# Three middle norms: later order of the second half, and the inverse root as ScalarE's square root and VectorE's reciprocal

## The reference

```python
def rms_norm(x, g):
    xf = x.astype(jnp.float32)
    y = xf * lax.rsqrt(jnp.mean(xf * xf, axis=-1, keepdims=True) + EPS)
    return (y * g.astype(jnp.float32)).astype(x.dtype)

    x = x + g1[:, None] * mix
    h2 = rms_norm(x, g_ffn_norm[l]) * (1.0 + sc2[:, None]) + sh2[:, None]
    u = causal_depthwise_conv(h2 @ w_up[l], w_conv[l], b_conv[l])
```

## Time and profile before

| what | value |
| --- | --- |
| median of 3 runs | 1750.63 us (1747.38 to 1750.98) |
| the profiled execution, its own time | 1747.48 us |
| its span | 1745.7 us, 32410 instructions |
| TensorE busy | 1691.8 us (97%) |
| VectorE busy | 1092.8 us (63%) |
| ScalarE busy | 744.8 us (43%) |
| GpSimd busy | 298.2 us (17%) |
| mean granted clock of TensorE | 0.994 |

### The profile page before, as it was taken

One profiled execution on the slowest core, in us unless ns is written; L12 is line 12 of the kernel. 1 busy time (PEld: TensorE's weight loads), 2 busy tenths in 40 slices (PEclk: granted clock), 3 DMA queues, 4 the chain that ended last, 5 costly groups with the idle time before them and its releaser, 6 DMA issues.

```text
span 1745.7 us, 32410 instructions
## 1 busy us (share of the span) xinstructions
PE 1691.8 (97%) x12781; PEld 1503.0 (86%) x12781; DVE 1092.8 (63%) x1748; ACT 744.8 (43%) x1111; POOL 298.2 (17%) x286
## 2 busy tenths in 40 slices
PE   5999999999999999899999999999999999999998
PEld 4876666788888888799999999999999999989986
DVE  6866586777664568855858664344753766754633
ACT  4467574455332342632323545446323643322323
POOL 2112296211000002532005221110102000000002
PEclk8999999999999999999999999999999999999999
DMA  9463532443333232263435752332543233332332
GB/s 313 122 145 97 161 114 80 130 91 113 95 91 105 85 103 69 79 182 118 132 102 156 225 142 87 99 117 80 166 117 96 74 96 90 91 97 85 96 95 75
DMA packets 321167, 201.18 MB, mean 115 GB/s; under 512 B 51279, under 2 KB 303814, under 8 KB 320918
## 3 DMA queue, kind: packets, MB, share of 16 engines
q1 hardware_dynamic: 300976, 160.79, 32.4%
q0 software_dynamic: 7952, 24.83, 4.7%
q10 hardware_dynamic: 12118, 13.88, 2.3%
HBM read 177.75 MB, written 17.24 MB: 112 GB/s over the span
## 4 chain that ended last, share of the span: by engine, by line
PE 84%; DVE 6%; ACT 4%; SPq 2%; issue 2%; DMA 1%; POOL 1%; ACTq 0%; DVEq 0%; POOLq 0%
PE ps L1467 69%; SPq L854 2%; PE ps L1769 1%; DVE wlo L2154 1%; PE ps L1608 1%; PE ps L1795 1%; PE ps L1779 1%; PE ps L1667 1%; PE ps L1999 1%; PE ps L1682 1%; PE ps L1584 1%; DVE acol L2229 1%; ACT whi L912 1%; DMA xrow<-in_x_dram 1%; PE ps L1925 0%
## 5 line engine op out<-in xcount | busy, mean ns | idle before, releaser
L1467 PE MATMUL ps<-zhi,whi 128*128 128x258 f32 (+2 forms) x2072 | 639.1, 308 | 1.4 <-ACT ub L1201 0.6
L1467 PE MATMUL ps<-zlo,whi 128*128 128x258 f32 (+2 forms) x2072 | 633.4, 306 | 0.0
L1467 PE MATMUL ps<-zhi,wlo 128*128 128x258 f32 (+2 forms) x2072 | 632.0, 305 | 0.0
L1467 PEld LDWEIGHTS ps<-zhi,whi 128*128 128x128 f32 x2072 | 390.8, 189 | 25.6 <-issue 2.2
L2154 DVE TENSOR_TENSOR wlo<-stage,whi 128x1024 fp32r<-128x1024 f32 x256 | 324.2, 1268 | 136.1 <-ACT whi L912 124.1
L1467 PEld LDWEIGHTS ps<-zlo,whi 128*128 128x128 f32 x2072 | 390.2, 188 | 19.5 <-issue 1.2
L1467 PEld LDWEIGHTS ps<-zhi,wlo 128*128 128x128 f32 x2072 | 390.8, 189 | 18.2
L912 ACT ACTIVATE whi<-stage 128x1024 fp32r<-128x1024 f32 x256 | 269.4, 1055 | 309.3 <-PE ps L1467 260.2
L1467 PE MATMUL ps<-ghi,whi 128*128 128x512 f32 x340 | 134.7, 396 | 0.0
L1467 PE MATMUL ps<-glo,whi 128*128 128x512 f32 x340 | 134.2, 395 | 0.0
L1467 PE MATMUL ps<-ghi,wlo 128*128 128x512 f32 x340 | 134.0, 394 | 0.0
(11 more groups left out here) (426 smaller groups left out, 2827.2 us busy)
## 6 DMA issues: line engine op xcount, KB each, us to landing
stage<-in_w_up_dram SPq DMA_DIRECT2D x88, 512.0 KB, 3.8
stage<-in_w_in_dram SPq DMA_DIRECT2D x74, 512.0 KB, 4.0
stage<-in_w_down_dram SPq DMA_DIRECT2D x32, 512.0 KB, 4.0
ring<-in_w_ada_dram POOLq DMA_DIRECT2D x24, 512.0 KB, 4.3
adab<-in_w_ada_dram SPq DMA_DIRECT2D x16, 512.0 KB, 8.0
stage<-in_w_down_dram SPq DMA_DIRECT2D x16, 384.0 KB, 3.4
stage<-in_w_o_dram SPq DMA_DIRECT2D x8, 512.0 KB, 4.0
ring<-in_w_ada_dram SPq DMA_DIRECT2D x8, 512.0 KB, 3.7
```

What stands on the lines that cost most here:

```text
L1467: last = pe.matmul(out, w(a, k), x(k, t0, t1), start=(k == 0 and a is whi and x is x_hi), stop=(k == ks - 1 and a is wlo))
```

## The change

In norms 3, 4 and 5 `rs` is no longer made by Ln and Exp on ScalarE: ScalarE takes the square root (`root_half`), VectorE the reciprocal of it in place. ScalarE's first z comes before the second half's square, and the second half's root behind z 2. VectorE adds the second half of the last residual behind zu 1 of the first half instead of ahead of the norm. TensorE makes the statistics of half 1 no longer behind the last job but in `first_pair`, behind the products of k = 0 and 1 of half 0 (`STAT_AT = 2`). The last norm (n = 6) keeps its order.

```diff
+STAT_AT = 2
@@ ScalarE
-            def log_half(n, h):
+            def root_half(n, h):
                 c = half(n, h)
                 act.wait_ge(stat_mm, STAT0[n] + h + 1)
-                act.activation(rs[:, c], ps[:, 4 + h, 0:c.stop - c.start], ACT.Ln, scale=1.0 / D, bias=small[:, 0:1])\
+                act.activation(rs[:, c], ps[:, 4 + h, 0:c.stop - c.start], ACT.Sqrt, scale=1.0 / D, bias=small[:, 0:1])\
                    .then_inc(rmid_done, 1)
-
-            def exp_half(n, h):
-
-                c = half(n, h)
-                act.wait_ge(rmid_done, 2 * (n - 3) + h + 1)
-                act.activation(rs[:, c], rs[:, c], ACT.Exp, scale=-0.5).then_inc(rs_done, 1)
@@ ScalarE
                 square_tile(n, 6)
-                act.activation(small[:, 60:61], small[:, 0:1], ACT.Ln)
+                act.activation(small[:, 60:61], small[:, 0:1], ACT.Sqrt)
                 square_last(n, 0)
-                log_half(n, 0)
-                exp_half(n, 0)
+                root_half(n, 0)
+                z_half(n, 0, 0)
                 square_last(n, 1)
-                for k in range(KD):
+                for k in range(1, KD):
                     z_half(n, 0, k)
-                    if k == 2:
-                        log_half(n, 1)
-                    elif k == 5:
-                        exp_half(n, 1)
+                    if k == STAT_AT:
+                        root_half(n, 1)
                 for k in range(KD):
                     z_half(n, 1, k)
@@ TensorE, last_job
-                half_stats(n, 1)
+                if n == 6:
+                    half_stats(n, 1)
@@ TensorE, first_pair
                     for k in range(KD):
+                        if (h, k) == (0, STAT_AT):
+                            half_stats(n, 1)
                         pe.wait_ge(zlo_done, nbase[n] + KD * h + k + 1)
@@ VectorE: residual_last(n, gate), a loop over both halves, becomes residual_half(n, gate, h), one half
-            def norm(n):
+            def norm(n, gate):
                 s = NORMS[n]
-                wait_residual(dve, RES[n], 8)
+                residual_half(n, gate, 0)
+                wait_residual(dve, RES[n], 7)
                 dve.wait_ge(res_half, n - 2)
@@ VectorE
                 for h in range(2):
+                    if h:
+                        wait_job_out(dve, J[RES[n]] + 7)
+                    dve.wait_ge(rmid_done, 2 * (n - 3) + h + 1)
+                    dve.reciprocal(rs[:, half(n, h)], rs[:, half(n, h)]).then_inc(rs_done, 1)
                     dve.wait_ge(rs_done, RS0[n] + h + 1)
                     for k in range(KD):
+                        if (h, k) == (0, 2):
+                            residual_half(n, gate, 1)
                         u, c = nbase[n] + KD * h + k, half(n, h)
```

More of the change, by code:

```diff
@@ L2155, in split_lo, with residual_half @@
                                   ALU.subtract).then_inc(split_done, 1)
-            def residual_last(n, gate):
+            def residual_half(n, gate, h):
                 job = J[RES[n]] + 7
[L2160 to L2173, removed]
-            def norm(n):
+                if h == 0:
+                    dve.wait_ge(half_mm, n - 2)
+                else:
+                    dve.wait_ge(marks, plan.full[job])
+                c = job_half(n, h)
+                off = 0 if n == 5 else META
+                x, o = xT[:, 7, off + c.start:off + c.stop], ps[:, 2 * (job % 2) + h, 0:c.stop - c.start]
+                if gate is not None:
+                    ins = dve.scalar_tensor_tensor(out=x, in0=o, scalar=mod[:, gate + 7:gate + 8], in1=x,
+                                                   op0=ALU.mult, op1=ALU.add)
+                else:
+                    ins = dve.tensor_tensor(x, o, x, ALU.add)
+                ins.then_inc(emptied[job % 2] if h else res_half, 1)
+            def norm(n, gate):
                 s = NORMS[n]
-                wait_residual(dve, RES[n], 8)
+                residual_half(n, gate, 0)
+                wait_residual(dve, RES[n], 7)
                 dve.wait_ge(res_half, n - 2)
@@ L2495, in _ @@
                     residual(J["wo"] + j, T1, 16, j, None, 0)
-            residual_last(3, 16)
-            norm(3)
+            norm(3, 16)
             read_mod(5)
@@ L2516, in ffn @@
                                 residual(job0 + j, T, f["g2"], j, None, 0)
-                        if c == 2:
-                            residual_last(4, f["g2"])
                         continue
@@ L2528, in ffn @@
                                 rows_out(j - 2)
-                        residual_last(6, None)
+                        residual_half(6, None, 0)
+                        residual_half(6, None, 1)
                         rows_out(6)
@@ L2702, in _ @@
             ffn(0)
-            norm(4)
+            norm(4, FFNS[0]["g2"])
             link(dve.memset(S5[:, :, :, 0:1], 0.0))
@@ L2961, in _ @@
                     residual(J["out"] + j, T3, None, j, None, 0)
-            residual_last(5, None)
-            norm(5)
+            norm(5, None)
             ffn(1)
```

## The result

The changed kernel takes 1761.11 us (median of 6 runs), the kernel before 1750.34 us beside it: ratio 1.0057 [1.0047, 1.0067]. The forecast was 1760.8 us with a range of 1755 to 1766. The profiled execution takes 1761.44 us (span 1759.6); before it was 1747.48 (1745.7).

A forecast was written before the change was run, and what follows sets the result against it. TensorE, busy 97% of the span, was taken to bound the kernel. Chains of 2.48, 2.73 and 2.54 us (7.75) plus 2.4 for clock falls gave 10.15, added to the median 1750.63: 1760.8 us, range 1755 to 1766.

The forecast's parts named there:

- The first root: First half, norm 3: load 1.28 and Exp 0.42 removed, reciprocal of 1.79 us added; first `zu` 0.08 later.
- The two waits: Around the first reciprocal: 0.02 us between Sqrt and reciprocal, 0.23 between reciprocal and first `zu`.
- The order behind it: Norm 3, first half: first product 0.5 us later; z 3 waits for the later second statistics, low 3 1.40 later.
- The second root: Between low 7 and second half's first `zu`: reciprocal plus wait adds 2.02 us on VectorE; norm 3's 48 products start 2.48 later.
- The clock: TensorE's clock falls to half at two of norms 3 to 5 behind one long idle stretch, 1.2 us each, 2.4 us.
- The sum: Whole kernel: chains 7.75 us plus clock 2.4 us, 10.15 us slower, added to the median of 1750.63.
- That the clock doesn't fall: Rival at norms 3 to 5: TensorE's clock stays up, only +7.75 us, 1758.4 us; chance 0.20.
- Twice a norm: Rival: clock falls also at the 2 us pause before the second half, +15.9 us, 1766.5 us; chance 0.07.
- A dear reciprocal: Rival: VectorE's reciprocal takes 2.8 us, two a norm, +6.2 us on top of the forecast, 1767 us; chance 0.07.
- loads that stay: Rival: Identity or Square needs another table than Sqrt, four loads a norm on the path, +15 us; chance 0.02.
- the prediction's sign of no load: Sign on ScalarE: no table load between the square of tile 6 and the end of the norm.
- The cheap one: Rival between Sqrt and first `zu`: cheaper reciprocal, each 0.1 us off takes 0.6 us from the whole; 1750.3 at 0.49; chance 0.10.

The follow-up runs named there:

- the root behind z 5: Changed kernel with ScalarE making the second half's root behind z 5 instead of behind z 2: 1754.41 us, 1.0015 to the kernel before.
- filling products: Unread products of constants added in TensorE's idle stretch before each norm's first product; seven in the changed kernel: 1758.99 us, ratio 1.0043 to before.
- with seven: Changed kernel with second root behind z 5 and seven added products of constants in TensorE's idle stretch: 1751.42 us, ratio 1.0003 to before.
- the multiply: Changed kernel with each VectorE reciprocal replaced by a multiplication by 1/256 of the same shape (`rs` no inverse root): 1748.77 us, ratio 0.9988 to before.
- the old order: Changed kernel's square root and reciprocal, but second residual and statistics ahead of the first `zu` as before: 1755.13 us, ratio 1.0028 to before.
- the one function: Changed kernel with root behind z 5 and ScalarE's Abs_reciprocal_sqrt in place of Sqrt and reciprocal: 1745.04 us, ratio 0.9965 to before.
- Three products in the gap: Changed kernel with root behind z 5, ScalarE's Abs_reciprocal_sqrt and three added products of constants in TensorE's idle stretch: 1744.12 us, ratio 0.9963 to before.
- Ten of them: Changed kernel with ten added products of constants in TensorE's idle stretch of each norm: 1763.38 us, ratio 1.0067 to before.
- GpSimd's power: Changed kernel with second reciprocal as GpSimd's power of -1, root behind z 4, seven added products of constants: 1875.91 us, ratio 1.0709 to before.

## Why the prediction was right

**The first root: right.** The reciprocals took 1.74 to 1.80 us for the 1.79 to 1.85 forecast, by the line through two short rows. From 32 columns to 256 the slope is (1.75 - 0.353) / 224 = 6.2 ns a column. The estimate from the Trainium skill (VectorE: DVE Perf Modes, "First, the fixed hardware budget"), 2.1 us, is not borne out; the measurement decides. (Six times 2.1 less 1.79 would also have added 2 us to the sum, and not the 2.4 that the prediction gives.) The two waits were guessed the wrong way round: 0.14 between Sqrt and reciprocal, 0.03 between reciprocal and `zu`, for 0.02 and 0.23. `zu` came 0.03 earlier instead of 0.08 later: the load removed is paid back in full.

**The order behind it: right, a little too dear.** The second statistics lie behind the twelve products, and z 3 waits for them in `root_half`; the kernels with the root behind z 5 show that this alone costs about 1.3 us a norm with the clock up (1.31 at norm 3 without filling products; 1.27, 1.35 and 1.32 with seven). Low 3 came 1.19 later for 1.40: the first product 0.14 sooner than forecast, and the statistics 0.59 instead of 0.67.

**The second root: right, 0.24 too dear.** The reciprocal stands in VectorE's row and TensorE idles 1.79 us. The term was 2.02 and came to 355.09 - 353.31 = 1.78 by the row below, since behind a reciprocal in VectorE's own row there is no wait of 0.23 (353.31 is the reciprocal's start on VectorE's timeline; the chain counts it from the end of low 7, 0.08 later). This is the mis-sized term: 0.24 here and 0.21 at low 3 make the difference between 2.48 and 2.03. Summed over the norms the chains came to 6.43 (with the clock up) for 7.75.

```profile
353.31 1.74 DVE L2188 RECIPROCAL rs<-rs 128x256 f32<-128x256 f32 x1
```

**The clock: right in kind and number.** It fell at two of three norms. It cost 0.97 and 1.67, 2.64 us for the 2.4 forecast. The mean had been taken at 1.2; norm 5 was dearer since the clock was down at the first product already (0.55 us long for 0.36). The Trainium skill (TensorE: Matmul & The Clock Gate, "Why this matters for your kernels") says that an idle gap between bursts of matmuls, if it is long enough, drops the clock to half. Norms 4 and 5 agree (gaps of 3.59 and 3.11 us). Norm 3 doesn't fit a rule by length alone: the clock stayed up over 3.22 us, longer than norm 5's, and the measurement decides.

**The sum: right, partly by errors that cancel.** Chains 1.3 too dear, the clock 0.2 too cheap: 9.1 in the norms for 10.15. The medians differ by 10.8; by the ratio it is 10.0, interval 8.2 to 11.7, which holds the 9.1. What lies beyond the norms wasn't tied to the change: in the profiled pair it lies in code that is the same, and how much of it repeats stays open. That the median came within 0.3 us of the forecast is luck.

**The rivals.** That the clock doesn't fall: false at norms 4 and 5. Twice a norm: not seen; behind the statistics of norm 4 it rose (0.95 over the stretch from 735), and it is 1.00 from 737 to 748, over the second pause. A dear reciprocal and loads that stay: false, with 1.77 us, and a single load left in the norm. It comes right behind the square of tile 6 (at 338.23, ahead of a Sqrt of one column), where the kernel before has one too; the three behind the first root are gone. Read to the letter, the prediction's sign of no load from that square on was wrong by this one. The cheap one was false, but its price of 0.6 us for each tenth was right, as the multiply showed at norm 3.

## What to carry to other kernels

An operation that is moved from an idle engine to the one that sets the pace can cost its whole duration, even where it replaces one about as long: of the 1.7 us of the second load and Exp only 0.94 had held VectorE up, of the reciprocal in its own row all 1.78 did. A step that is moved behind other work on one engine has to be moved on the engine that waits for it, too: one changed line, the root behind z 5, gave back more than 4 us. And look first for a function that does both steps in one: the inverse root on ScalarE made three norms shorter, where Sqrt and reciprocal had made them longer.

## What the runs showed that I had not expected

- Whether TensorE's clock falls doesn't go by the length of the last wait alone. It stayed 1.00 over 3.22 us at norm 3, and fell at norm 3 with the old order behind 1.12 and then 2.43 us of idle time with the statistics between, at norm 4 behind 2.83 with the one function, and at norm 5 behind 3.11. What tells these apart stays open.
- A fall of the clock needn't cost anything. With the new root and the old order it fell at norm 3 too, and VectorE's row alone makes up that norm's +1.72.
- Three products in the gap (with the one function) or seven (with the reciprocal) kept it at 1.00 in every norm, at no cost where they ended ahead of the real product. Ten of them ran into it.
- ScalarE's inverse root takes the 0.47 us of Sqrt at 256 columns, and no table load came between it, Square and Identity.
- GpSimd's power takes 42.9 us for 256 columns, some 168 ns a column; VectorE's reciprocal takes 1.75.
- In the old order the reciprocal waited 1.5 us behind a residual that had cost nothing before. A new instruction also inherits the waits of what stands ahead of it in its engine's row.
